# Putting six query tiles' weight products among the units of the third attention

## The reference

```
proj = h @ w_in + b_in
q, k, v = split(proj, [16 * 64, (16 + 2) * 64])
q = q.reshape(B, nb, 128, 2, 8, 64)      # 2 groups of 8 heads, blocks of 128 queries
s = einsum('bnqkgd,bnskd->bnkgqs', q, kb) * 64 ** -0.5   # keys: previous block and own
mx = maximum(max(s), sink); e = exp(s - mx)
p = e / (sum(e) + exp(sink - mx))
o = einsum('bnkgqs,bnskd->bnqkgd', p, vb)
return o.reshape(B, T, 1024) @ w_out + b_out
```

## Time and profile before

| | before |
|---|---|
| median of 3 runs | 2469.01 us (2467.21 to 2470.68) |
| span of the profiled execution | 2468.0 us |
| what lies around that span, against the median | 1.0 us |
| PE busy | 2423.7 us, 98% |
| ACT busy | 1079.6 us, 44% |
| POOL busy | 972.3 us, 39% |
| DVE busy | 936.0 us, 38% |

### The profile page before, as it was taken

How to read it: one execution, slowest core, us unless ns; L and a number is a source line. 1 busy time by engine, 2 the same in 40 slices (tenths; PEclk the granted TensorE clock), 3 DMA queues, 4 the chain that set the end, 5 groups by cost and what they waited for, 6 DMA issues and landing times.

```text
span 2468.0 us, 36248 instructions
## 1 busy us (share of the span) xinstructions
PE 2423.7 (98%) x11990; PEld 2004.0 (81%) x11990; DVE 936.0 (38%) x2051; ACT 1079.6 (44%) x1917; POOL 972.3 (39%) x484
## 2 busy tenths in 40 slices
PE   8999999999999999999999999999999999999998
PEld 6888888888778978888887978788888797788886
DVE  7976322211477753222214243321211773311212
ACT  7565443432347754444335534432332583432321
POOL 4821444444331124444443413444443423444441
PEclk9999999999999999999999999999999999999999
DMA  4300333333420013233332312233333202233331
GB/s 154 116 30 18 90 97 101 94 102 105 128 69 10 1 35 94 93 102 93 103 102 79 103 39 81 77 95 95 100 94 94 69 18 69 86 101 95 94 94 68
DMA packets 57866, 202.75 MB, mean 82 GB/s; under 512 B 7072, under 2 KB 7968, under 8 KB 57392
## 3 DMA queue, kind: packets, MB, share of 16 engines
q1 hardware_dynamic: 54864, 196.02, 26.2%
q10 hardware_dynamic: 2912, 5.55, 0.6%
HBM read 199.44 MB, written 2.10 MB: 82 GB/s over the span
## 4 chain that ended last, share of the span: by engine, by line
PE 41%; issue 14%; POOL 7%; ACT 1%; DVE 1%; POOLq 0%; DVEq 0%; ACTq 0%
PE bank L764 36%; POOL w_lo L618 7%; PE bank L1008 1%; PE bank L967 1%; PE bank L979 1%; ACT h_hi L1492 1%; PE bank L1372 0%; PE bank L1353 0%; ACT gained L1495 0%; PE bank L1367 0%; PE bank L793 0%; PE bank L1055 0%; PE bank L881 0%; PE bank L770 0%; PE bank L786 0%
## 5 line engine op out<-in xcount | busy, mean ns | idle before, releaser
L618 POOL TENSOR_TENSOR w_lo<-w_raw,w_hi 128x1024 fp32r<-128x1024 f32 x368 | 883.3, 2401 | 1197.7 <-ACT w_hi L1449 1188.1
L764 PE MATMUL bank<-h_hi,w_hi 128*128 128x512 f32 x1648 | 650.5, 395 | 7.2 <-DVE tmp L2476 2.1
L764 PE MATMUL bank<-h_lo,w_hi 128*128 128x512 f32 x1648 | 642.2, 390 | 0.0
L764 PE MATMUL bank<-h_hi,w_lo 128*128 128x512 f32 x1648 | 642.2, 390 | 0.0
L1449 ACT ACTIVATE w_hi<-w_raw 128x1024 fp32r<-128x1024 f32 x368 | 386.8, 1051 | 242.7 <-PE bank L764 214.0
L764 PEld LDWEIGHTS bank<-h_hi,w_hi 128*128 128x128 f32 x1648 | 309.8, 188 | 82.3 <-issue 5.9
L764 PEld LDWEIGHTS bank<-h_hi,w_lo 128*128 128x128 f32 x1648 | 309.7, 188 | 65.2
L764 PEld LDWEIGHTS bank<-h_lo,w_hi 128*128 128x128 f32 x1648 | 309.9, 188 | 65.0 <-issue 2.2
L764 PE MATMUL bank<-mact_hi,w_hi 128*128 128x512 f32 x512 | 199.3, 389 | 1.7 <-DVEq L2342 1.7
L764 PE MATMUL bank<-mact_hi,w_lo 128*128 128x512 f32 x512 | 199.2, 389 | 0.0
L764 PE MATMUL bank<-mact_lo,w_hi 128*128 128x512 f32 x512 | 199.2, 389 | 0.0
(11 more groups left out here) (403 smaller groups left out, 3489.3 us busy)
## 6 DMA issues: line engine op xcount, KB each, us to landing
w_raw<-in_weights SPq DMA_DIRECT2D x368, 512.0 KB, 3.6
out<-x ACTq DMA_DIRECT2D x8, 256.0 KB, 2.1
x<-in_xT SPq DMA_DIRECT2D x4, 256.0 KB, 6.8
x<-in_xT ACTq DMA_DIRECT2D x4, 256.0 KB, 7.4
memx<-in_memT SPq DMA_DIRECT2D x1, 1024.0 KB, 9.8
cmp_w1k<-in_cmp_w ACTq DMA_DIRECT2D x1, 1024.0 KB, 5.6
cmp_w1v<-in_cmp_w ACTq DMA_DIRECT2D x1, 1024.0 KB, 7.5
rope_c<-in_rope_c SPq DMA_DIRECT2D x1, 256.0 KB, 8.4
```

What stands on the lines that cost most here:

```text
L618: nc.gpsimd.tensor_tensor(w_lo[:, t % RING, :], w_raw[:, t % RAW, :], w_hi[:, t % RING, :].bitcast(F32), ALU.subtract).then_inc(lo_ready, 1)
L764: r = nc.tensor.matmul(out, a, b, start=first and n == 0, stop=last and n == 2)
```

## The change

1. Only `sq0` (bank 2) and `sq1` (bank 3) are made before the attention. The 48 product steps of `sq2` to `sq7` (`query_products`), all in bank 1, are put among the units: four before the first scores, four between the first four scores, and one in each of steps n = 0 to 39, between the transposes and the values. The first product step of a tile waits until DVE has moved the tile before out of bank 1 (`query_moved`).
2. The scores have three banks (2, 3, 0) instead of four, and run four units ahead instead of five.
3. DVE moves tile 2 + n/8 at the end of its step n when n is a multiple of 8, and makes the remainders of its two heads in the next steps but one (`rest_of_query`); ACT rounds them two steps earlier, with the bias in the same operation (`round_query`), and rounds one weight chunk where n is 4 more than a multiple of 8. The factor 1/8 goes to the keys.
4. POOL's staging copies, `q_stage2` and the filler matmuls are gone; the scores read `q_swa`. POOL makes the remainder of one weight chunk, in one whole operation, behind the sinks of heads 0, 2, 4, 6, 8 and 10.
5. The stream is written out rather than looped.

```
+OWN.update({"sq0": 2, "sq1": 3}, **{f"sq{j}": 1 for j in range(2, KT)})
-    return 5 if kind.startswith("swa") else 4
+LOOK_AHEAD = 4
+def swa_unit(n):
+    return (f"swa{n // 32}", 0, n % 8, n % 32 // 8) if n < 64 else None
+def query_step(s):
+    return f"sq{2 + s // KT}", s % KT
+QUERY_STEPS = (KT - 2) * KT
+EARLY_STEPS = 8
 def bank_of(kind, u, i=0):
+    if kind.startswith("swa"):
+        return (32 * int(kind[3]) + 8 * i + u) % 3
```

GpSimd:

```
+            end = CHUNK["sq1"] + AHEAD + 1
+            rests(start, end)
+            for head in range(2 * SWA_PAIRS):
+                add_sink(*swa_unit(TT * head))
+                if head in (0, 2, 4, 6, 8, 10):
+                    rest(end)
+                    end += 1
+            start = norms(end, ["mlppre1"])
```

The tensor block, in `scores`:

```
+                if kind.startswith("swa") and u % TT == 0:
+                    pe.wait_ge(q_split, 24 + heads_before(kind, u) + 2 * i + 1)
-                    pe.wait_ge(probs_ready, g - kind.startswith(("dsa", "mem0", "swa")) + per * i)
+                    pe.wait_ge(probs_ready, g - kind.startswith(("dsa", "mem0")) + per * i)
```

The tensor block, in the last layer:

```
-                    for j in range(1, KT):
-                        column_tile(f"sq{j}")
+                    t = CHUNK["sq1"]
+                    chunk_ready(t)
+                    for k in range(KT):
+                        r = three(of("sq1")[:, :], slot(t, k), (h_hi[:, k, :], h_lo[:, k, :]), k == 0, k == KT - 1)
+                    r.then_inc(chunks_used, 1)
+                    def query_products(s):
+                        name, k = query_step(s)
+                        if k == 0:
+                            chunk_ready(CHUNK[name])
+                            pe.wait_ge(query_moved, int(name[2]) if s else 1)
+                        r = three(of(name)[:, :], slot(CHUNK[name], k), (h_hi[:, k, :], h_lo[:, k, :]), k == 0, k == KT - 1)
+                        if k == KT - 1:
+                            r.then_inc(chunks_used, 1)
+                    for s in range(4):
+                        query_products(s)
                     pe.wait_ge(k_split, 13)
-                    attention_stream(pe, STREAMS[2], lambda at: attention_begin(at, banks_free), pair_of_heads)
+                    for n in range(4):
+                        if n < 2:
+                            pe.wait_ge(query_moved, n + 1)
+                        scores(*swa_unit(n))
+                        query_products(4 + n)
+                    for n in range(2):
+                        transposes(*swa_unit(n))
+                    for n in range(2 * 4 * SWA_PAIRS):
+                        if swa_unit(n + LOOK_AHEAD):
+                            scores(*swa_unit(n + LOOK_AHEAD))
+                        if swa_unit(n + 2):
+                            transposes(*swa_unit(n + 2))
+                        if EARLY_STEPS + n < QUERY_STEPS:
+                            query_products(EARLY_STEPS + n)
+                        values(*swa_unit(n))
```

The scalar block:

```
+                    round_query(0)
+                    split_ahead(CHUNK["sq1"])
+                    round_query(1)
+                    for n in range(LOOK_AHEAD - 1):
+                        exponentials(*swa_unit(n))
+                    for n in range(2):
+                        move_transposed(*swa_unit(n))
+                    for n in range(2 * 4 * SWA_PAIRS):
+                        if swa_unit(n + LOOK_AHEAD - 1):
+                            exponentials(*swa_unit(n + LOOK_AHEAD - 1))
+                        if swa_unit(n + 2):
+                            move_transposed(*swa_unit(n + 2))
+                        done = 2 + n // 8
+                        if n % 8 in (1, 2) and done < KT:
+                            round_query(done, [n % 8 - 1])
+                        if n % 8 == 4 and done < KT:
+                            split_ahead(CHUNK[f"sq{done}"])
```

The vector block:

```
+                    scaled_by_root("sk", sk[:, :])
+                    biased(0, sk[:, :], col("swa_bk"), SCALE)
+                    scaled_by_root("sv", diag[:, :])
+                    biased(1, diag[:, :], col("swa_bv"))
+                    move_query(0)
                     rest_of_both(9, sk[:, :], *k_swa)
+                    rest_of_query(0)
+                    move_query(1)
+                    hold_sink(0, 0)
+                    for n in range(LOOK_AHEAD):
+                        maximum(*swa_unit(n))
+                    rest_of_query(1)
+                    for n in range(2 * 4 * SWA_PAIRS):
+                        if swa_unit(n + LOOK_AHEAD):
+                            maximum(*swa_unit(n + LOOK_AHEAD))
+                        output(*swa_unit(n))
+                        done = 2 + n // 8
+                        if n % 8 == 0 and done < KT:
+                            move_query(done)
+                        if n % 8 in (2, 3) and done < KT:
+                            rest_of_query(done, [n % 8 - 2])
```

More of the change, by code:

```diff
@@ L209, in attention_stream @@
             begin(lambda u: (kind, pair, u, 0))
-        unrolled = int(n == 0 and first is not None)
-        if unrolled:
-            first(per, lambda u: (kind, pair, u, 0) if u < per else (kind, pair, u - per, 1))
         if pairs > 1:
-            with eng.Fori(unrolled, pairs - 1) as i:
+            with eng.Fori(0, pairs - 1) as i:
                 pair_of_heads(per, lambda u: (kind, pair, u, i) if u < per else (kind, pair, u - per, i + 1))
@@ L1600, in attention_begin @@
             def attention_begin(at):
-                for u in range(look_ahead(at(0)[0]) - 1):
+                for u in range(LOOK_AHEAD - 1):
                     exponentials(*at(u))
@@ L1607, in unit_of_pair @@
             def unit_of_pair(u, at):
-                later = u + look_ahead(at(u)[0]) - 1
+                later = u + LOOK_AHEAD - 1
                 if at(later):
@@ L1982, in _, with round_query @@
                     move("svT", sv[:, :, :], of("svT")[:, :].rearrange("p (a n) -> p a n", a=TT))
[L1983 to L1996, removed]
+                    def round_query(j, heads=(0, 1)):
+                        act.wait_ge(query_moved, j + 1)
+                        for hh, (part, hi, _) in enumerate(both_heads("swa0", j, sq_q[:, j, :])):
+                            if hh in heads:
+                                bias = col("swa_b_q", j)[HD * hh:HD * hh + HD, :]
+                                nc.scalar.activation(hi, part, ACT.Identity, bias=bias).then_inc(q_rounded, 1)
+                    round_query(0)
[15 more added lines that the diff above has]
+                            split_ahead(CHUNK[f"sq{done}"])
                     concat("scat", 2)
@@ L2271, in attention_begin @@
             def attention_begin(at):
-                if at(0)[0] == "swa0":
-                    hold_sink(0, 0)
-                for u in range(look_ahead(at(0)[0])):
+                for u in range(LOOK_AHEAD):
                     maximum(*at(u))
@@ L2279, in unit_of_pair @@
             def unit_of_pair(u, at):
-                later = u + look_ahead(at(u)[0])
+                later = u + LOOK_AHEAD
                 if at(later):
@@ L2681, in pair_between_rests @@
[L2681 to L2684, removed]
-                                biased(last + 2, sq_q[:, last, :], col("swa_b_q", last), SCALE)
-                            elif u in (1, 2):
-                                rest_of_queries("swa0", last - 1, sq_q[:, last - 1, :], [u - 1])
-                            elif u in (5, 6):
-                                rest_of_queries("swa0", last, sq_q[:, last, :], [u - 5])
@@ new lines, in rest_of_query @@
+                    def rest_of_query(j, heads=(0, 1)):
+                        dve.wait_ge(query_moved, j + 1)
+                        for hh, (part, hi, lo) in enumerate(both_heads("swa0", j, sq_q[:, j, :])):
+                            if hh in heads:
+                                dve.wait_ge(q_rounded, 24 + 2 * j + hh + 1)
+                                bias = col("swa_b_q", j)[HD * hh:HD * hh + HD, :]
+                                nc.vector.scalar_tensor_tensor(lo, part, bias, hi.bitcast(F32), ALU.add, ALU.subtract).then_inc(q_split, 1)
```

75 lines of the change are left out of this document (25 added, 50 removed).

## The result

The changed kernel takes 2479.23 us (median of 5 runs, 2477.98 to 2481.8), the kernel before beside it 2467.21 (5 runs, 2464.96 to 2470.68). The ratio is 1.0049 [1.0037, 1.0062]: 12.0 us slower, where 8.5 were forecast.

What follows compares the result with a forecast made beforehand. PE, busy 98% of the span, was taken to be bound by its own instructions. Terms +0.7 + 5.5 - 1.2 + 3.5 = +8.5 us on the median of 2469.0 gave 2477.5 us, range 2466 to 2486.

Steps and rivals of the forecast that it cites:

- product steps: 48 product steps moved among the units: each costs about 0.69 to 0.70 us where it cost 0.68, +0.7 us.
- late exponentials: Units n < 40: ACT's roundings and chunks covered by a slack of over 1 us a step, so no cost.
- tiles' ends: At n = 8 to 32 a tile's first product step waits for DVE's move: four holes of 1.4 us, +5.5 us.
- start: Start of the third attention: holes of 5.0 us against 6.2 before, -1.2 us.
- last 24 units: From n = 40: shorter look-ahead, ACT's roundings and chunk, and POOL's remainder before a sink slow the units, +3.5 us.
- s: Start of the scores heading a tile's first step; DVE's move was to reach PE at s+1.9, PE ready at s+0.5.
- steady pace: Last 24 units: scores-to-transposes chain of 1.89 us fits the 1.94 us that two steps give, 0.05 us to spare.
- Order of the queues: POOL's remainders end before the sink copies and meet none of DVE's query remainders in the units: at nothing for n < 40.
- Loads hide under the products: Rival, faster: weight loads of values and scores run under product matmuls, saving 13.6 us, 2463.9 us; chance 0.12.
- Small holes: Rival, same: holes of 0.8 us at tiles' ends, a start of 3, a tail of +1; 2470.7 us; chance 0.24.
- The clock falls in the new holes: Rival, slower: PE's idle at the start lowers its clock, costing 3.2 us, 2480.7, or 2484 with another; chance 0.14.
- POOL holds DVE: Rival, slower: two of POOL's six whole remainders each hold a DVE operation, 2 x 2.1 us, 2481.7 us; chance 0.06.

Runs made afterwards that it cites:

- experiment 8: Experiment 7's kernel with each product step ahead of the transposes in its step: 2468.86 us, ratio 1.0004 to the kernel before.
- Experiment 1: Changed kernel with DVE's move of each query tile one place sooner, ahead of the output and the maximum: 2475.59 us, ratio 1.0031 to the kernel before.
- experiment 5: Changed kernel with the edits of experiment 1 and experiment 2 together: 2471.04 us, ratio 1.0018 to the kernel before.
- Experiment 10: The kernel before, unchanged, profiled once more: 2465.66 us, stage 96.28 us in place of 98.59.
- experiment 2: Changed kernel with POOL's six remainders behind the sinks of the odd heads instead of the even ones: 2479.17 us, ratio 1.0045 to the kernel before.
- experiment 6: Changed kernel with scores five units ahead and a fourth bank from unit 46 on: 2479.22 us in one run.
- experiment 7: Changed kernel with the edits of experiments 1, 2, 3 and 6 together: 2469.54 us, ratio 1.0009 to the kernel before.
- experiment 9: Experiment 8's kernel with the last tile's weight chunk (ACT's rounding and POOL's remainder) left until after the stream: 2467.69 us, ratio 0.9999 to the kernel before.
- experiment 11: Experiment 9's kernel with POOL's second remainder after the first query remainders: 2467.3 us, ratio 1.0001 to the kernel before.
- experiment 4: The kernel before with scores four units ahead in place of five in the third attention, four banks kept: 2471.42 us, ratio 1.0016 to the kernel before.
- experiment 3: Changed kernel with ACT loading the exponential's table before rounding the second query tile: 2477.95 us, ratio 1.0039 to the kernel before.

## Why the prediction was right, and where its sizes were off

The mechanism held: the moved products hide nothing, and the time is lost at places that can be named. Seven edits closed most of them one after the other, 12.6 us of stage in all (109.46 to 96.90). The balance of the last version against the kernel before is then small on both sides: product steps +0.7 (48 x 0.015), four tiles' ends at 0.42 (12.48 - 2 x 6.03), +1.7, a tail of 20.58 for 18.84, +1.7, and a start that loses some 0.8 (13.56 us for 12.74 of work) where before lost 3.9, -3.1. That is +1.0; the stages say +0.6. The rival theory, products dear among units by themselves, falls with the steps that take the same 1.60 us in both orders (experiment 8).

By its terms, measured against a stage without the clock's fall (109.46 - 96.28 = 13.2; medians 12.0):

| Term | forecast | measured | from |
|---|---|---|---|
| product steps | +0.7 | +0.6 | 40 x (0.695 - 0.68) |
| late exponentials | nothing | +1.4 | 5 x 0.27 |
| tiles' ends | +5.5 | +5.3 | 4 x 1.33 |
| start | -1.2 | +1.2 | 5.1 against 6.2 - 2.3 |
| last 24 units | +3.5 | +4.9 | 23.7 against 18.84 |
| sum | +8.5 | +13.4 | |

The last row but one holds 0.2 that is work and not loss: the scores of one more unit come behind the values of unit 40, as they run four ahead and not five. The forecast of 2477.5 us lies nearer to the 2479.23 measured than its sum deserves: it was built on 2469.01 us for the kernel before, a median of three runs, and two more runs brought that to 2467.21.

- **Product steps.** Right: 0.70 where nothing waits, in the steps with eight loads and in the head of experiment 8.
- **Late exponentials.** A term put at nothing. For n < 40 ACT's two roundings and its chunk were to be covered by a slack of over 1 us a step. They are not quite: ACT makes them ahead of exponentials whose transposes stand in front of a step's products, and PE waits 0.04 to 0.16 us a time, 1.4 in all. Experiment 8 puts the products in front and the waits are gone.
- **Tiles' ends.** Right in place, releaser, order and size: first product at s + 1.78 in place of s + 1.9, hole 1.33 in place of 1.4. Experiments 1 and 5 close it to 0.23.
- **Start.** The loss after was hit (5.1 for 5.0), in part by luck: its waits were recorded as 0.58, 0.05, 1.15 and 1.51 us for the 0.9, 0.45, 1.3 and 2.2 forecast, with one of 0.58 that was not. The error is in the kernel before, and it is the term that was mis-sized most: of its 6.2 us, 3.2 were put down to the clock, and they stood as a property of the kernel that the change would remove. Experiment 10 has the stage without the fall, 2.3 us shorter.
- **Last 24 units.** Each of the three causes is there: POOL's late sink (0.94, experiment 2), look-ahead (1.6 alone, 0.88 beside the sink edit, experiments 6 and 7), the last chunk (1.30, experiment 9). They add to 3.1, and the tail of 9 and 11 is still 1.74 longer than before. All of that lies in its first two heads, 8.32 us for 6.50 from the values of unit 40 to those of unit 48 in experiment 11, where PE's transposes wait for ACT twice:

```profile
2017.79 0.44 PE L1007 MATMUL bank<-ident,tmp 128*128 128x128 f32 x2 [0.34 <-ACT tmp L1634]
...
2020.19 0.41 PE L1007 MATMUL bank<-ident,tmp 128*128 128x128 f32 x2 [0.60 <-ACT sq L1649]
```

ACT's two roundings of the last query tile stand just ahead of what they wait for (2016.57 and 2018.37, 0.7 us each), as the forecast had it; no experiment moved them, so this cause is read from the trace alone. The steady pace for which the forecast saw 0.05 us to spare is not held: experiment 4 puts four units of look-ahead at 0.55 a head.

- **Order of the queues.** That POOL's remainders cost nothing for n < 40 held for the changed kernel, and only there: the reciprocal's wait of 1.44 was covered by the output and maximum in front of the move. Experiment 1 took the cover away, and 0.43 a tile appeared.

The rivals. *Loads hide under the products*: a pace below 1.4 us a unit was wanted, 1.57 (6.27 / 4) came. PE's weight loads in a product step of the changed kernel:

```profile
2023.43 0.19 PEld L775 LDWEIGHTS bank<-h_lo,w_hi 128*128 128x128 f32 x1
2023.67 0.19 PEld L775 LDWEIGHTS bank<-h_hi,w_lo 128*128 128x128 f32 x1
2023.90 0.65 PEld L1024 LDWEIGHTS bank<-sv,sq 128*128 128x128 f32 x4
```

Each starts within 0.1 us behind the start of the matmul before its own, and the first value load at the last product's 2023.90: one ahead, never more. The partial reorder window of the Trainium skill (TensorE: Matmul & The Clock Gate, its table of the engine), which pulls weight loads ahead of running matmuls, is not seen to reach further here. *Small holes*: holes of 1.33, a start of 5.1 and a tail of 4.9 refute it. *The clock falls in the new holes*: 1.00 all through the stage in the profiled execution of the changed kernel, 0.89 in the first tile of experiment 6's, where it fell as the wait of 1.5 us before that tile ended, so it happens in some executions, for 1.6 us. *POOL holds DVE*: it does so at the keys, 7.01 us for four operations of 0.7, which the forecast had as part of the start. The trace agrees with the Trainium skill (SBUF — State Buffer, SBUF: two separate sides): by its rule a GpSimd operation and one of VectorE with two SBUF inputs exclude each other for a whole instruction. 7.01 less 2.8 is 4.2, two waits of about 2.1; with one of the two remainders moved away, 4.94 and one wait are left.

## What to carry to other kernels

Where the bounding engine is bound by its own instructions, moving work among others fills nothing; it only adds places where it can wait. Before moving it, write out for each new wait what stands ahead of its releaser in that engine's queue: 1.1 of the 1.33 us lost at a tile's end came from two operations put before a move, and from a sink queued behind a remainder. And repeat the profile of the kernel before: a fall of the clock in it may be of that execution only.

## What the runs showed of the hardware

- **The clock's fall differs between executions.** One kernel, one stretch, PE idle as long before it: 0.75 in one execution, 1.00 in another. Single times follow the mean granted clock: runs of the kernel before (23 beside experiments 9 to 11) have medians of 2471.4 us at 0.995 (6 runs), 2467.8 at 0.998 (5) and 2465.2 at 0.999 (8). Of its 68 runs 15 had 0.995; of 87 runs of the other kernels none, so how often it falls may well hang on the kernel. That is the likely reason why medians differ by less than stages: at equal clocks (0.999) experiment 4 is 6.8 us above the kernel before (2471.2 to 2464.4, the runs beside experiments 1 to 4), where the medians say 3.0. That it is the whole reason was not shown.
- **One start-to-start distance can mislead.** Behind a 128-wide matmul the second product starts 0.31 us after the first (2023.35 to 2023.66), behind a 256-wide one 0.24 (1971.21 to 1971.45). But the first starts 0.03 us after the transpose before it there, and 0.12 after the score matmul here: 0.34 and 0.35 together. A whole step with eight loads takes 1.60 us either way.
- **The profile's idle time can understate a hole.** In experiment 8 the wait reads 0.21 us, while a tile with it takes 0.42 more than two heads without; in the changed kernel it reads 1.11 for 1.33; in experiment 5 nothing for 0.23. Start-to-start distances over whole steps are the surer measure.
